# Splitting the second unit's weights ahead of the residual's norm, and the token-root matmuls inside that unit

## The reference

```python
for l in range(DEPTH_2):
    ng = norm_gains[l]
    x = x + FFN_RES_WEIGHT * rms_norm(swiglu(rms_norm(x, ng[0]), ffn_w_gu[l, 0], ffn_w_down[l, 0]), ng[1])
    h = rms_norm(x, ng[2])
    ...  # retention mixer (l = 0) or latent attention (l = 1), and attention over a memory
    x = x + rms_norm(mix, ng[3])
    x = x + FFN_RES_WEIGHT * rms_norm(swiglu(rms_norm(x, ng[4]), ffn_w_gu[l, 1], ffn_w_down[l, 1]), ng[5])
```

## Time and profile before

| | |
|---|---|
| Median of 3 runs | 1471.68 us (1465.82 to 1477.27) |
| The profiled execution | 1464.06 us, span 1462.3 us |
| Mean granted TensorE clock | 0.987 |
| TensorE busy | 1393.1 us (95%), 11538 matmul instructions |
| VectorE busy | 915.9 us (63%) |
| ScalarE busy | 723.5 us (49%) |
| GpSimd busy | 192.8 us (13%) |
| Chain that ended last | TensorE 79%, VectorE 9%, ScalarE 7% |

### The profile page before, as it was taken

One profiled execution on the slowest core, in us unless ns is written; L12 is line 12 of the kernel. 1 busy time (PEld: TensorE's weight loads), 2 busy tenths in 40 slices (PEclk: granted clock), 3 DMA queues, 4 the chain that ended last, 5 costly groups with the idle time before them and its releaser, 6 DMA issues.

```text
span 1462.3 us, 28144 instructions
## 1 busy us (share of the span) xinstructions
PE 1393.1 (95%) x11538; PEld 1347.5 (92%) x11538; DVE 915.9 (63%) x1312; ACT 723.5 (49%) x1149; POOL 192.8 (13%) x210
## 2 busy tenths in 40 slices
PE   5889899899999999998998999999999988899998
PEld 5877789899999999998898999999999977899997
DVE  7997776666545666447765666456564467656544
ACT  7812745545334554445446455445444465645443
POOL 0465000022100111013101111011110010111100
PEclk9999899999999999999999999999999999999999
DMA  9222424455554555544432555444555441255551
GB/s 371 104 108 91 153 87 143 175 202 199 178 199 146 202 199 200 190 174 148 145 145 89 204 197 215 176 171 173 184 203 190 157 171 58 104 190 196 190 199 58
DMA packets 36814, 244.33 MB, mean 167 GB/s; under 512 B 4208, under 2 KB 5360, under 8 KB 8816
## 3 DMA queue, kind: packets, MB, share of 16 engines
q1 hardware_dynamic: 34992, 238.17, 44.7%
q10 hardware_dynamic: 1728, 4.81, 1.0%
HBM read 241.67 MB, written 1.05 MB: 166 GB/s over the span
## 4 chain that ended last, share of the span: by engine, by line
PE 79%; DVE 9%; ACT 7%; issue 3%; POOL 2%; DMA 1%; SPq 0%; ACTq 0%; DVEq 0%; POOLq 0%
PE ps L1894 45%; PE ps L1936 26%; DVE wlo L1090 4%; ACT whi L599 2%; ACT ahi L851 1%; PE ps L2124 1%; ACT junk L866 1%; PE ps L2150 1%; DMA xtok<-in_xt 1%; POOL pr L1811 1%; PE ps L2140 1%; POOL pr L1812 1%; PE ps L1952 1%; ACT pP L789 1%; PE ps L2029 1%
## 5 line engine op out<-in xcount | busy, mean ns | idle before, releaser
L1090 DVE TENSOR_TENSOR wlo<-raw,whi 128x1024 fp32r<-128x1024 f32 (+1 forms) x434 | 506.5, 1209 | 265.9 <-ACT whi L599 265.6
L1894 PE MATMUL ps<-ahi,whi 128*128 128x256 f32 x2112 | 596.9, 283 | 31.5 <-DVE wlo L1090 26.1
L599 ACT ACTIVATE whi<-raw 128x1024 fp32r<-128x1024 f32 (+1 forms) x434 | 427.1, 1032 | 354.8 <-PE ps L1936 191.7
L1894 PE MATMUL ps<-alo,whi 128*128 128x256 f32 x2112 | 589.6, 279 | 0.0
L1894 PE MATMUL ps<-ahi,wlo 128*128 128x256 f32 x2112 | 589.5, 279 | 0.0
L1894 PEld LDWEIGHTS ps<-ahi,whi 128*128 128x128 f32 x2112 | 399.6, 189 | 40.0 <-issue 24.1
L1894 PEld LDWEIGHTS ps<-alo,whi 128*128 128x128 f32 x2112 | 399.3, 189 | 0.7 <-issue 0.7
L1894 PEld LDWEIGHTS ps<-ahi,wlo 128*128 128x128 f32 x2112 | 399.7, 189 | 0.0
L1832 POOL TENSOR_TENSOR hlo<-fh,hhi 128x256 f32 (+3 forms) x104 | 85.5, 822 | 745.9 <-ACT hhi L906 535.2
L1541 DVE TENSOR_TENSOR fa<-ps,r 128x512 f32<-128x512 f32 x104 | 72.0, 692 | 167.4 <-PE ps L1894 167.2
L1936 PE MATMUL ps<-whi,hhi 128*128 128x256 f32 x960 | 152.3, 279 | 0.0
(11 more groups left out here) (350 smaller groups left out, 1343.4 us busy)
## 6 DMA issues: line engine op xcount, KB each, us to landing
raw<-in_w_gu SPq DMA_DIRECT2D x88, 1024.0 KB, 4.8
raw<-in_w_fd SPq DMA_DIRECT2D x44, 1024.0 KB, 4.8
raw<-in_w_up SPq DMA_DIRECT2D x16, 1024.0 KB, 4.8
raw<-in_w_dn SPq DMA_DIRECT2D x16, 1024.0 KB, 4.8
raw<-in_w_ret SPq DMA_DIRECT2D x13, 1024.0 KB, 4.8
raw<-in_w_mg SPq DMA_DIRECT2D x8, 1024.0 KB, 4.9
raw<-in_w_o SPq DMA_DIRECT2D x8, 1024.0 KB, 5.7
raw<-in_w_mem SPq DMA_DIRECT2D x4, 1024.0 KB, 4.8
```

Of the source, the lines that this page charges most:

```text
L599: nc.scalar.activation(whi[:, m % SPL, c], raw[:, n % RAW, c], ACT.Copy).then_inc(S("w_hi"), 1)
L1090: ins = tt(wlo[:, m % SPL, c], raw[:, n % RAW, c], whi[:, m % SPL, c].bitcast(F32), ALU.subtract)
L1894: ins = mm(dst, lhsT, rhs, start=k == 0 and p == 0, stop=k == kt - 1 and p == len(pairs) - 1)
```

## The change

Four edits, and no instruction more or less. ScalarE and VectorE each call `ahead(LAST_DOWN[q])` inside the transition, between `high` or `low` and the squares or the reciprocal, so that unit 1's weights are split there. The calls that did it before find it done. On TensorE `token_roots(q)` moves from behind unit 0 into the middle of unit 1, between its two output tiles, in all seven places.

```diff
@@ ScalarE, transition(q)
                 high(0)
                 high(1)
+                ahead(LAST_DOWN[q])
                 for t in range(TT):
                     act.wait_ge(S("x_new"), 4 * q + 2 * t + 2)
@@ TensorE
-            def products(outs, n, high, low, kt, tokens=False, need=None):
+            def products(outs, n, high, low, kt, tokens=False, need=None, halfway=None):
 ...
                 for c, dst in enumerate(outs):
+                    if halfway and c:
+                        halfway()
                     for k in range(kt):
@@ TensorE, ffn
                 def hidden(i, u):
-                    unit(up + u, ahi, alo, KT, i, need=need if i is None and u == 0 else None)
-                    if i is None and u == 0:
-                        token_roots(q)
+                    unit(up + u, ahi, alo, KT, i, need=need if i is None and u == 0 else None,
+                         halfway=(lambda: token_roots(q)) if i is None and u == 1 else None)
@@ TensorE, retention
                 unit(AT["w_ret", 12], ahi, alo, KT, need=need)
-                token_roots(2)
-                ret_unit(3)
+                ret_unit(3, lambda: token_roots(2))
@@ TensorE, latent
                 unit(u2, ahi, alo, KT, need=need)
-                token_roots(5)
-                unit(u1, ahi, alo, KT)
+                unit(u1, ahi, alo, KT, halfway=lambda: token_roots(5))
```

More of the change, by code:

```diff
@@ L1899, in n_slot, with unit @@
                 return SPLIT_BEFORE[n] % SPL
-            def unit(n, high, low, kt, i=None, tokens=False, need=None):
+            def unit(n, high, low, kt, i=None, tokens=False, need=None, halfway=None):
                 g = GROUP[n]
@@ L1909, in unit @@
                 bank = two(g % 2)
-                products([bank[:, 0], bank[:, 1]], n, high, low, kt, tokens, need=need)
+                products([bank[:, 0], bank[:, 1]], n, high, low, kt, tokens, need=need, halfway=halfway)
             def acts_need():
@@ L2214, in retention, with ret_unit @@
             def retention():
-                def ret_unit(c):
-                    unit(AT["w_ret", c], ahi, alo, KT, tokens=6 <= c < 9)
+                def ret_unit(c, halfway=None):
+                    unit(AT["w_ret", c], ahi, alo, KT, tokens=6 <= c < 9, halfway=halfway)
                 def rotations(p):
```

## The result

The changed kernel took 1463.93 us (median of 20 runs, 1459.29 to 1470.43), beside it the kernel before 1470.21 (20 runs, 1464.43 to 1483.05): ratio 0.9948, 95% interval 0.9928 to 0.9967. In two later comparisons the same two kernels stood at 0.9992 [0.9974, 1.0010] and 0.9981 [0.9960, 1.0002], both without a difference clear of noise. The forecast was 1465.8 and "within 1%". So the time of the first comparison came out as said. The traces say that half of the reasons were right; the rest of this text is on the other half.

A forecast was written before the change was run, and what follows sets the result against it. TensorE, nearly always busy, loses 8.4 us in seven waits for VectorE's low weight halves. Gains of 5.0 + 0.4 + 0.5 = 5.9 us took the median 1471.68 to 1465.8, range 1457.5 to 1472, within 1% at 0.95.

The forecast's parts named there:

- The wait at the five plain hand-overs: Hand-overs 0, 1, 3, 4, 6: TensorE's 0.90 us wait for unit 1's low half goes, gaining 1.0 us each.
- 5.0 us: Sum over hand-overs 0, 1, 3, 4 and 6 at 1.0 us each; bounds 4.5 and 5.3.
- Hand-over 2: Into retention: VectorE's chain limits the gain to 0.4 us, bounds -1.7 and 0.7, with `pos_i` and `dpm` issued later.
- The wait for `pP`: TensorE's 1.73 us wait at 686.42, behind hand-over 2, was to grow as TensorE arrives earlier.
- Hand-over 5: Into the latent block: TensorE's 2.13 us wait goes, the `lsq` wait takes nearly all; gain 0.5 us, bounds 0 and 1.2.
- The fall at 1184.70: Half-clock stretch until 1188.10 behind hand-over 5's 2.13 us wait, costing 1.7 us; it was to go with that wait.
- The clock rival: Longer idle at 677 to 686 or ahead of 1199.98 drops the clock: 1469.2; opposite sign 1464.1; chance 0.1 together.
- The slower rival: Hand-over 2: `pos_i` or `dpm` lands late against the weight load, deciding from 11.6 us after issue; 1478.3; chance 0.05.
- The sum: Whole kernel: 5.0 + 0.4 + 0.5 = 5.9 us gained, bounds 2.8 and 7.2.

The follow-up runs named there:

- before's second execution: The kernel before, unedited, traced once more against itself; 1465.41 us, ratio 0.9991 [0.9966, 1.0017], 12 runs.
- the filler: The changed kernel plus 36 matmuls of 256 columns with unused results ahead of TensorE's wait for `lsq`; 1463.05 us, ratio 0.9984 to the kernel before.
- the quarter with the loads first: Changed kernel with small matmuls a quarter into unit 1 and ScalarE issuing hand-over 2 and 5 loads ahead of `high`; 1461.68 us, 0.9968 to before.
- with filler: The quarter with the loads first, plus 24 matmuls with unused results ahead of the wait for `lsq`; 1460.58 us, ratio 0.9965 to the kernel before.

## Why the prediction was right and wrong

- **The wait at the five plain hand-overs: right.** All seven rows behind `wlo` are gone, slacks within 0.1 us of the working, nothing took their place; 1.13 us at equal spacing against 1.0. (Hand-over 0: 1.24 against the mean of before's two executions, 1.14 against the second, which had after's spacings there.)
- **"5.0 us" as their sum: wrong.** The term held for the wait, and not for the time. The step that failed is that a matmul costs the same before and after, which the sum takes without saying so. With the spacing that each execution drew, four hand-overs gave 0.35 each and the first 1.24, so 2.6 us. Two traces of before are few for that average.
- **Hand-over 2: right in size and mostly in mechanism.** `rkT` is awaited until 25.43 us behind the transposes, 25.96 before: 0.53 gained, 0.4 forecast. `pos_i` was the late one, by 0.36 us; it stood behind the weight load and took no turns with it. The wait for `pP` stayed at 1.70. The segment mean is 138.37 against 138.67: 0.3.
- **Hand-over 5: the chain right against one execution, the sum wrong.** `cqg` came 20.74 us behind the transposes and not 21.51, `lsq` 0.77 earlier (forecast 0.5), the fall at 1184.70 went, the wait grew to 4.70 (forecast about 5). Against before's second execution, with `cqg` at 19.90 and `lsq` at 28.41, both come 0.8 later. The step that failed is the bounds, "0 and 1.2": the clock was put into the gain only. The fall at 1184.70 was not in before's second execution at all, though TensorE waited the same 2.1 us ahead of unit u1 there; so the gain from its going was a gain over one execution. The segments of after are 1.5 to 3.6 us over the mean of before's two (93.35), so the term is -2.8, not +0.5.
- **The clock rival** named the place ("some 5 us ahead of 1199.98") and was given less than 0.1, on the ground that the work behind the wait is paced by others. The traces speak against this: L2128 takes 2.08 us at 0.50 and, with the filler, 1.14 at 1.00. One stretch was priced; in two of three executions there was three times its length.
- **The slower rival** did not happen: 5.4 us to landing against the 11.6 that it needed.
- **The sum.** 2.6 + 0.3 - 2.8 is nothing, as in the sums of the segments. The medians of the first comparison lie 6.3 us apart, those of the two later ones 0.1 and 2.5; it is before's that moved (1470.21, then 1465.35 and 1464.19). What each kernel lost in the unchanged first 280 us and the drawn spacings could move a median so, but that they did it in the first comparison is not shown: it has one trace of each kernel, and there the first 280 us speak against the change. The mean size of the gain remains open between nothing and 6 us. That the forecast's 5.9 hit the first comparison is luck: the term of 5.0 gave 2.6 and the term of 0.5 gave -2.8.

The best version is the quarter with the loads first: 0.9968 [0.9943, 0.9992], with filler 0.9965 [0.9944, 0.9986]. The filler adds nothing there that can be told (segments 92.00 and 92.09). These intervals overlap those of after (0.9981 and 0.9992), so that it is better than after rests on the segments.

## What to carry to other kernels

When a change lets TensorE arrive earlier at a chain that it does not set, the wait there grows, and the clock behind a longer wait has to be priced as a possible loss in the sum and not as an afterthought; shorten that chain in the same change (here the loads issued ahead of `high`, and the small matmuls a quarter into the unit). Price a removed wait at equal matmul spacing, count matmuls in windows before trusting the difference of two executions, and multiply each run's time by its mean granted clock to see what is left of its scatter. And look first at the stretch ahead of the first edit: what differs there is the noise.

## What the runs showed that was not expected

- Two spacings, 113.3 and 117.8 ns, for the same stream of matmuls at a granted clock of 1.00, each for a whole phase. For comparison, the Trainium skill, TensorE: Matmul & The Clock Gate, section "Back-to-back issue gap", gives N / 2.4 + 2.5 ns for an isolated matmul of N columns, by which an estimate for 256 columns is 109.2 ns. It says that the spacing in a stream with a weight load for each matmul is set by both; both spacings here lie above the estimate.
- The first 280 us, unchanged, lost between 8.5 and 17.1 us to the half clock, from one execution to the next; their end came between 279.6 and 287.8 us.
- Behind a wait of 4.70 us the granted clock stayed at 0.50 for 10.1 us in two executions and for 6.8 in a third of the same kernel; with waits of 1.6 to 1.8 us it was 3.4 us. A wait of 2.1 us ahead of unit u1 was followed by 3.4 us at half clock in one execution of before and by none in the other.
- Two small loads on ScalarE's queue, issued 0.6 us behind a 1 MB load on SyncE's, moved nothing for the first 2.6 us and landed behind it, while the 1 MB load took its usual 4.8 us.
